# Projections moved behind the mixers, with the head norms inside them; first queries inside the output norms; the recurrence's vector work in halves

## The reference

```python
def _merge_ab(m, o, a, norm_w, w_out):                # end of layer 0's mixer
    hm = _head_norm(m, norm_w).astype(o.dtype) * jax.nn.sigmoid(o)
    cat = jnp.concatenate([hm, a.reshape(a.shape[0], a.shape[1], A_Q)], -1)
    return cat @ w_out
def _merge_c(h, g, norm_w, w_out):                    # end of layer 1's mixer
    return (_head_norm(h, norm_w).astype(g.dtype) * jax.nn.silu(g)) @ w_out
...
x = _layernorm(DEEPNORM_ALPHA * x + g1 * y_lat, ln_w[layer, 0], ln_b[layer, 0])
f_lat = _peer(x * (1.0 + sc2) + sh2, ...)             # its queries: q = hb @ wq
...
def rg_lru_mixer(zb, conv_w, conv_b, w_r, b_r, w_i, b_i, lam):
    ...
    log_a = -LRU_C * r.astype(jnp.float32) * jax.nn.softplus(-lam.astype(jnp.float32))
    a = jnp.exp(log_a)
    inp = jnp.sqrt(-jnp.expm1(2.0 * log_a)) * (i * xb).astype(jnp.float32)
    ...                                                # h = a * h_before + inp, along the tokens
    return jax.nn.gelu(gate) * h.astype(gate.dtype)
def ssd_mixer(...):
    xbc = jax.nn.silu(causal_dwconv(xbc, conv_w, conv_b))
```

## Time and profile before

| | value |
|---|---|
| median of 3 runs | 3676.08 us (3673.44 to 3679.04) |
| profiled execution / its span | 3676.99 / 3675.2 us |
| mean granted clock of TensorE | 0.938 |
| PE busy | 3006.5 us, 82% |
| DVE busy | 1954.0 us, 53% |
| ACT busy | 830.8 us, 23% |
| POOL busy | 880.6 us, 24% |
| DMA | 1024.09 MB, mean 279 GB/s; 403 to 427 GB/s in the bulk of the PEER layers |

### The profile page before, as it was taken

How to read it: one execution, slowest core, us unless ns; L and a number is a source line. 1 busy time by engine, 2 the same in 40 slices (tenths; PEclk the granted TensorE clock), 3 DMA queues, 4 the chain that set the end, 5 groups by cost and what they waited for, 6 DMA issues and landing times. The chain is left out here.

```text
span 3675.2 us, 28126 instructions
## 1 busy us (share of the span) xinstructions
PE 3006.5 (82%) x8564; PEld 1485.9 (40%) x8564; DVE 1954.0 (53%) x5001; ACT 830.8 (23%) x2149; POOL 880.6 (24%) x773
## 2 busy tenths in 40 slices
PE   6997788888888888777888777888877779898898
PEld 3443443333333333333343543333332536453663
DVE  1136657777777777677710756777776331222101
ACT  0112412222222222222312512222222130121100
POOL 0000004444444444444400004444444000000000
PEclk8997799999999999999999889999999899898999
DMA  5143129999999999999922439999999333333343
GB/s 200 58 147 129 63 92 427 427 427 426 427 427 423 423 423 420 424 421 417 403 97 92 156 135 427 427 427 426 427 427 411 133 126 119 106 115 115 115 148 115
DMA packets 242859, 1024.09 MB, mean 279 GB/s; under 512 B 46582, under 2 KB 51190, under 8 KB 142342
## 3 DMA queue, kind: packets, MB, share of 16 engines
q0 software_dynamic: 110592, 805.36, 52.2%
q1 hardware_dynamic: 131688, 215.68, 16.7%
q10 hardware_dynamic: 432, 1.31, 0.1%
HBM read 1021.15 MB, written 1.13 MB: 278 GB/s over the span
## 5 line engine op out<-in xcount | busy, mean ns | idle before, releaser
L1526 PE MATMUL l_peer_experts_acc<-l_peer_experts_ring,l_peer_experts_diag 128*128 128x512 f32 x1840 | 866.9, 614 | 208.3 <-ACT l_peer_experts_diag L1584 207.6
L1526 PE MATMUL l_peer_experts_acc<-weight_slots,l_peer_experts_diag 128*128 128x512 f32 x1232 | 588.9, 621 | 152.4 <-ACT l_peer_experts_diag L1584 151.9
L1745 DVE SCALAR_TENSOR_TENSOR l_peer_experts_ring<-l_peer_experts_ring,h_tiles 128x1024 f32<-128x1024 f32 x460 | 563.3, 1225 | 277.5 <-DMA l_peer_experts_ring<-in_expert_rows,l_peer_experts_picks 273.9
L1453 POOL DMA_INDIRECT l_peer_experts_ring<-in_expert_rows,l_peer_experts_picks x460 | 528.7, 1149 | 616.7 <-PE l_peer_experts_acc L1526 540.9
L1453 POOL DMA_INDIRECT weight_slots<-in_expert_rows,l_peer_experts_picks x308 | 350.7, 1139 | 1303.3 <-DVE l_peer_experts_picks L1674 875.0
L1526 PEld LDWEIGHTS l_peer_experts_acc<-l_peer_experts_ring,l_peer_experts_diag 128*128 128x128 f32 x1840 | 340.3, 193 | 703.9 <-issue 406.7
L1745 DVE SCALAR_TENSOR_TENSOR weight_slots<-weight_slots,h_tiles 128x1024 f32<-128x1024 f32 x308 | 377.1, 1224 | 184.0 <-DMA weight_slots<-in_expert_rows,l_peer_experts_picks 180.5
L1526 PEld LDWEIGHTS l_peer_experts_acc<-weight_slots,l_peer_experts_diag 128*128 128x128 f32 x1232 | 230.9, 196 | 487.0 <-issue 282.1
L1577 ACT ACTIVATE l_peer_experts_gel<-l_peer_experts_dots 128x2 f32<-128x2 f32 x384 | 78.2, 204 | 1183.9 <-DVE l_peer_experts_ring L1745 712.0
L1584 ACT ACTIVATE l_peer_experts_diag<-const_ident,l_peer_experts_wgt 128x128 f32<-128x128 f32 x768 | 266.3, 394 | 238.5 <-DVE l_peer_experts_wgt L1691 223.9
L1478 PE MATMUL l_peer_experts_queries<-h_t,l_query_weights 128*128 128x512 f32 (+3 forms) x576 | 182.3, 462 | 4.2 <-PEq L61 4.2
(11 more groups left out here) (459 smaller groups left out, 3336.8 us busy)
## 6 DMA issues: line engine op xcount, KB each, us to landing
weight_slots<-in_w_mod SPq DMA_DIRECT2D x24, 2048.0 KB, 7.6
weight_slots<-in_w_in SPq DMA_DIRECT2D x20, 2048.0 KB, 7.6
l_query_weights<-query_weights SPq DMA_DIRECT2D x16, 1024.0 KB
weight_slots<-in_w_mlp_up SPq DMA_DIRECT2D x8, 2048.0 KB, 7.7
weight_slots<-in_w_mlp_down SPq DMA_DIRECT2D x8, 2048.0 KB, 7.6
weight_slots<-in_gla_w_in SPq DMA_DIRECT2D x6, 2048.0 KB, 7.7
weight_slots<-in_ab_w_in SPq DMA_DIRECT2D x5, 2048.0 KB, 8.8
l_peer_experts_ring<-in_expert_rows,l_peer_experts_picks POOLq DMA_INDIRECT x460
```

Of the source, the lines that this page charges most:

```text
L1453: pool.indirect_dma_start(rows(b, k, None), None, uv, bass.IndirectOffsetOnAxis(ap=picks[:, b % 4, k:k + 1], axis=0)).then_inc(landing(b, ...
L1526: ins = nc.tensor.matmul(acc[:, b % 2, c * BANK:(c + 1) * BANK], diag[:, k % DIAGS, :], row[:, c * BANK:(c + 1) * BANK], start=(k == 0), s ...
L1745: nc.vector.scalar_tensor_tensor(row, row, 1.0, h[:, tile_of(b), :], ALU.mult, ALU.mult, accum_out=dots[:, b % 2, k:k + 1]).then_inc(dotte ...
```

## The change

It does five things.

1. ab_qkv (and its weight tiles) comes behind the mLSTM rather than ahead of it, and carries the mLSTM's head norm as a side (`head_norm_parts`, new, the same operations as `stage_head_norm`). The stage ab_norm is gone. ab_qkv's evictions are now ACT's alone.
2. c_g comes behind the GLA, takes silu in its evictions, and carries the GLA's head norm. Behind its last matmul it multiplies by the gate (four pieces of 512 columns on DVE) and does the 16 transposes and their 4 copies itself. The stages c_norm and c_turn are gone.
3. `stage_out_norm` computes head 0's query for the first token tile (16 matmuls of 128x128 and two copies into a new buffer) ahead of the transposes of the tile before the last but one (layer 0: tile 2 of 4) or of the last (layer 1). `stage_peer` begins with `score(0)`, and `project` at unit 2.
4. The SSD convolution's taps and bias are loaded in b_xbc rather than b_z; SP waits there until they have landed.
5. `lru_parts` takes 1 - a*a = -(a*a + 1) tanh(log_a), so it has no reciprocal, and does all of it in two halves of 4 of the 8 groups. Both roots come ahead of b_za's last eviction; tanh and exp of the first half come one part earlier.

TensorE's list around the end of layer 1's mixer, first before the change, then after. `gla_` is the GLA, `c_g_acc` the gate's projection, `c_turn_` and `c_g_turned` the transposes, `c_out_` the output projection with its norm; a branch ends a stage or opens one.

```diff
-    both = func is None and len(groups(BANK)) > 1 and side is None
+    both = func is None and len(groups(BANK)) > 1 and side is None and turned_out is None
...
+                if turned_out:
+                    for i, (t, m) in enumerate(quads):
+                        pe.wait_ge(made, i + 1)
+                        if i >= 4:
+                            pe.wait_ge(emptied, i - 3)
+                        for k in range(4):
+                            at = t * BANK + k * P
+                            last = nc.tensor.transpose(turn_ps[:, i % 4, k, :], turn_src[:, m, at:at + P], ident)
+                        last.then_inc(turned, 1)
...
+                        act.wait_ge(turned, i + 1)
+                        nc.scalar.activation(turn_dst[:, 4 * t:4 * t + 4, m * P:(m + 1) * P], turn_ps[:, i % 4, :, :], ACT.Copy).then_inc(emptied, 1)
...
+                    make_link = Link(dve, make_chain)
+                    for i, (t, m) in enumerate(quads):
+                        if m == 0:
+                            dve.wait_ge(act_out, t + 3)
+                        make(make_link, m, slice(t * BANK, (t + 1) * BANK)).then_inc(made, 1)
...
+                def query():
+                    wq, wq_loaded, count, _ = queries
+                    pe.wait_ge(wq_loaded, count)
+                    pe.wait_ge(emptied, quads_of(0)[-1] + 1)
+                    pe.wait_ge(gated, n - 1)
+                    for half in range(2):
+                        for k in range(KC):
+                            last = nc.tensor.matmul(acc[:, 0, half, 0:P], wq[:, 0, k, half * P:(half + 1) * P], h_t[:, k, 0:P], start=(k == 0), stop=(k == KC - 1))
+                        last.then_inc(queried, 1)
                 for i in range(max(n - 2, 0), n):
+                    if i == max(n - 2, 1):
+                        query()
                     turn(i)
             @block.scalar
@@ -754,6 +802,11 @@
                     root(i)
                     copy(i - 2)
                 for i in range(max(n - 2, 0), n):
+                    if i == max(n - 2, 1):
+                        for half in range(2):
+                            act.wait_ge(queried, half + 1)
+                            nc.scalar.activation(queries[3][:, 0, half, 0:P], acc[:, 0, half, 0:P], ACT.Copy)
                     copy(i)
...
+    def scalar(act):
+        if gate is not None:
+            for m in tiles:
+                nc.scalar.activation(gate[:, m, :], gate[:, m, :], gate_func).then_inc(gated, 1)
+        for i in range(len(tiles)):
+            act.wait_ge(ss_ready, i + 1)
+            nc.scalar.activation(rs[:, i, :], ss[:, i, :], ACT.Sqrt).then_inc(rs_ready, 1)
...
+    return {"sync": sync, "scalar": scalar, "vector": vector}, normed
...
-                first_head = project(0, before, 1)
-                for _ in range(2):
-                    next(first_head)
+                pe.sem_inc(q_done, 2)
+                first_head = project(2, before, 1)
                 score(0)
...
-                take(0, 4)
+                act.sem_inc(q_taken, 2)
+                take(2, 4)
...
+def early_conv_parts(nc, st, w, b, wc, bc):
+    loaded = st.sem("conv_loaded")
+    def sync(sp):
+        load_conv(sp, w, b, wc, bc, loaded)
+        sp.wait_ge(loaded, 80)
+    return [{"sync": sync}]
...
-        dve.wait_ge(tanh_ready, 1)
-        link(nc.vector.tensor_scalar(den[:, :, :], th[:, :, :], -1.0, 1.0, ALU.mult, ALU.add))
-        link(nc.vector.reciprocal(den[:, :, :], den[:, :, :]))
-        nc.vector.scalar_tensor_tensor(th[:, :, :], th[:, :, :], -2.0, den[:, :, :], ALU.mult, ALU.mult).then_inc(root_in, 1)
-        dve.wait_ge(root_out, 1)
-        link(nc.vector.tensor_tensor(i_t[:, :, :], i_t[:, :, :], th[:, :, :], ALU.mult))
...
+        def logs(g):
+            dve.wait_ge(emptied, HALF * (g + 1))
+            for h in range(HALF * g, HALF * g + HALF):
+                last = nc.vector.tensor_scalar(r[:, h, :], r[:, h, :], cols[:, 4, h:h + 1], None, ALU.mult)
+            last.then_inc(loga_ready, 1)
+            link(nc.vector.tensor_tensor(some(i_t, g), some(i_t, g), some(x, g), ALU.mult))
+        def squares(g):
+            dve.wait_ge(a_ready, g + 1)
+            link(nc.vector.tensor_tensor(some(den, g), some(r, g), some(r, g), ALU.mult))
+            dve.wait_ge(tanh_ready, g + 1)
+            nc.vector.scalar_tensor_tensor(some(th, g), some(den, g), 1.0, some(th, g), ALU.add, ALU.mult).then_inc(root_in, 1)
+        def scans(g):
+            dve.wait_ge(root_out, g + 1)
+            link(nc.vector.tensor_tensor(some(i_t, g), some(i_t, g), some(th, g), ALU.mult))
+            for h in range(HALF * g, HALF * g + HALF):
+                last = nc.vector.tensor_tensor_scan(den[:, h, :], r[:, h, :], i_t[:, h, :], 0.0, ALU.mult, ALU.add)
+            link(last)
+            link(nc.vector.tensor_tensor(some(gate, g), some(gate, g), some(den, g), ALU.mult))
+        logs(0)
+        squares(0)
+        logs(1)
+        squares(1)
+        scans(0)
+        scans(1)
+    g0, g2, g4, g6 = (gates(h) for h in range(0, GROUPS, 2))
+    return [{"sync": sync, "scalar": decay}, g0, g2, g4, {"tensor": g6["tensor"], "scalar": lambda act: (g6["scalar"](act), powers(0)(act))},
+            {"scalar": powers(1), "vector": vector}, {"scalar": root(0)}, {"scalar": root(1)}]
...
-    some(a["ab_w_in"][0], ("ab_v", 2 * M_W, M_W), ("ab_qk", 0, 2 * M_W), ("ab_o", 3 * M_W, M_W), ("ab_qkv", qkv, A_Q + 2 * A_KV))
+    some(a["ab_w_in"][0], ("ab_v", 2 * M_W, M_W), ("ab_qk", 0, 2 * M_W), ("ab_o", 3 * M_W, M_W))
     some(a["w_mod"][0], ("mod0_rest", 2 * D, 4 * D))
+    some(a["ab_w_in"][0], ("ab_qkv", qkv, A_Q + 2 * A_KV))
...
-            stage_linear(nc, "ab_qkv", weights, h_t, tiles, qkv)
             stage_mlstm(nc, qk_t, v_aug, g_cols, m_rows, consts["sel"], consts["far"], hm, weights, (*mod0, mod_out))
+            stage_linear(nc, "ab_qkv", weights, h_t, tiles, qkv,
+                         side=lambda st: [head_norm_parts(st, hm, range(TT), H_M, P, a["ab_norm_w"][0], cat, LN_EPS, o, ACT.Sigmoid)[0]])
             stage_attention(nc, qkv, consts["cos"], consts["sin"], consts["bars"], a["ab_sink"][0], consts["ident"][:, :], cat, weights, (*mod1, mod_out))
-        stage_head_norm(nc, "ab_norm", hm, range(TT), H_M, P, a["ab_norm_w"][0], o, ACT.Sigmoid, cat, LN_EPS, weights)
-        stage_transpose(nc, "ab_turn", consts["ident"][:, :], cat, h_t, range(TT), KC)
+        stage_transpose(nc, "ab_turn", consts["ident"][:, :], cat, h_t, range(TT), KC, weights=weights)
...
-            stage_linear(nc, "c_g", weights, lat_t, token_tiles(LT), g)
             stage_gla(nc, wl, up, bias, h_t, q_t, k_t, v, consts["sees"], consts["ident"][:, :], *scratch, hc, weights, (*mod1, mod_out))
-        stage_head_norm(nc, "c_norm", hc, range(LT), H_C, DV_C, a["gla_norm_w"][0], g, ACT.Silu, hc, LN_EPS, weights)
-        stage_transpose(nc, "c_turn", consts["ident"][:, :], hc, h_t, range(LT), KC)
+        def gated(link, m, cols):
+            return nc.vector.tensor_tensor(hc[:, m, cols], hc[:, m, cols], g[:, m, cols], ALU.mult)
+        stage_linear(nc, "c_g", weights, lat_t, token_tiles(LT), g, func=ACT.Silu,
+                     side=lambda st: [head_norm_parts(st, hc, range(LT), H_C, DV_C, a["gla_norm_w"][0], hc, LN_EPS, weights=weights)[0]],
+                     turned_out=(gated, hc, h_t, consts["ident"][:, :]))
...
+                                     + early_conv_parts(nc, st, a["ssd_conv_w_2"][0], a["ssd_conv_b_2"][0], *conv))
```

133 lines of the change are left out of this document (91 added, 42 removed).

## The result

The changed kernel's four runs took 3620.86, 3623.09, 3632.12 and 3632.14 us, median 3627.61, against 3676.31 for four runs of the kernel before: a ratio of 0.9866 (95% interval 0.9845 to 0.9887). Four more runs of it in a later series gave 3618.09 to 3629.40 (ratio 0.9853, 0.9836 to 0.9869). Forecast were 3616.4 us and a range of 3605 to 3629. So it is faster, as said, and the size is 49 us where 60 were forecast. The profiled execution, 3620.86 us with a span of 3619.1, is the second shortest of the eight, so all_again's profile further down is the fairer picture of the usual execution.

The account below looks back on a forecast made before the run. PE is 82% busy, but its idle gaps at stage starts and ends were taken as the cost. Gains sum to 59.7 us, from 3677.0 to 3617.3 profiled, 3616.4 for the median; range 3605 to 3629.

Parts of the forecast that it names:

- ab_qkv behind the mLSTM, 13.3: Attention's end to ab_turn: removing ab_norm, its head norm hidden under ab_qkv's matmuls, gains 13.3 us, bounds 11 to 15.
- 0.4 of half clock: Cost of 0.4 us counted against the moved ab_qkv for running at half clock.
- c_g behind the GLA, 11.0: GLA's end to c_out: norm, gate and transposes inside the moved c_g, gaining 11.0 us, bounds 9 to 14.
- c_out's own start then falls 0.7 short in clock: Start of c_out after the moved c_g: 0.7 us lost to a lower clock.
- First queries, 4.6 and 4.6: Starts of both PEER layers: head 0's query computed inside the output norms gains 4.6 us in each layer.
- Taps a stage earlier, 7.9 and 1.0: Convolution beside b_z: earlier start gains 7.9 us, and b_g's start after a shorter idle 1.0 more.
- Recurrence, 17.3: Tail ahead of b_wb: no reciprocal, work in halves; gains 17.3 us, bounds 15 to 18.5.
- DVE then ends at about 3014: Recurrence's tail: DVE's last work ends at about 3014, with the last eviction ending at 3013.0.
- (a): Rival, PEER layers: gathers set the ends, so the earlier first score gives nothing; 3625.6 us, chance 0.08.
- (b): Rival, recurrence: ACT's single queue makes PE or DVE wait, so the tail remains; 3631 us, chance 0.05.
- (c): Rival, b_xbc: the taps' element loads delay SP's weight loads or the gated MLP's; 3620 to 3625 us, chance 0.06.
- (d): Rival, moved ab_qkv and c_g: PE stays at clock 0.50, matmuls take twice as long; 3681 us, slower, chance 0.03.

Follow-up runs that it names:

- all_again: The changed kernel run once more with nothing edited: median 3627.34 us, profiled execution 3629.40 us.
- undo_ab: The changed kernel with ab_qkv ahead of the mLSTM and ab_norm a stage of its own, as before: 3636.82 us.
- late_only: The changed kernel with ab_qkv, c_g and first queries all undone, keeping only the recurrence and the earlier taps: 3655.54 us, ratio 0.9937 to the kernel before.
- undo_gate: The changed kernel with c_g ahead of the GLA and c_norm and c_turn as stages of their own, as before: 3634.06 us.
- undo_queries: The changed kernel with head 0's first queries computed in both PEER layers again, as before: 3635.08 us.
- best: logs_first plus, in layer 0, a second early query for token tile 1 in ab_out and the first exp ahead of the copies: 3618.76 us, ratio 0.9833.
- undo_taps: The changed kernel with the convolution's taps and bias loaded in b_z, as before: 3630.98 us.
- logs_first: The changed kernel with both halves' logarithms on DVE ahead of the first half's squares: 3621.29 us, ratio 0.9853 to the kernel before.
- before_again: The kernel before, unchanged, run and profiled a second time: 3677.17 us over ten runs, ratio 1.000.

## Why the prediction was right, and where a term was mis-sized

The mechanism of each of the five edits was right and four of their own gains came close. Most of the shortfall of 11 us is in the clock of stages that the change doesn't touch, which the prediction allowed for in its range (5 us either way) but had at nothing in its sum; 1.9 are the recurrence's. That the total still lies in the range is owed to that allowance, not to having sized it.

1. *ab_qkv behind the mLSTM, 13.3.* The 14.7 of ab_norm went, as the 2.05 us show. The term itself was sized well: 12.5 to 14.2, in the mean 13.0, once the stages that the edit leaves alone are taken out (undo_ab). All but ab_qkv gives 13.8, less than 1 us off the 14.7; ab_qkv itself is at 44.2 to 44.6 us in eight of ten profiles where it was 43.2, and at 42.9 in two, so the "0.4 of half clock" was 1.0 to 1.3 in most and nothing in some. What was missing stands beside the term: the stretch as a whole gains 14.5 and 7.5 in the two profiles of the changed kernel, since in all ten the mLSTM is 1.7 to 5.0 longer. late_only and undo_ab, with the longest one (89.6) in the old order, show that this doesn't come from the order.
2. *c_g behind the GLA, 11.0.* 38.7 against 38.8 worked out, 12.1 of gain up to c_out (10.5 against undo_gate, the GLA left out). The step "c_out's own start then falls 0.7 short in clock" was too small: c_out without the query (undo_queries) takes 42.0 rather than 40.3, 1.7. That makes 10.4. Since this cost and the query's don't add (undo_gate), the split between this term and the next is one choice of two; together c_out is 3.4 longer, where 2.1 to 2.7 were forecast. The windows of its start, before and changed:

```profile
2137.00:2141.00 4.00, 3.24 (x8) 1.59 (x9) 0.00 (x0) 1.28 (x1) 0.00 (x0) 1.00 0.51 182
```

```profile
2110.00:2114.00 4.00, 3.25 (x4) 1.36 (x5) 0.00 (x0) 1.28 (x1) 0.00 (x0) 0.61 1.05 385
```

It begins at 1.00 behind a long idle and 16 transposes that ran at 0.50 (2132.6 to 2136.4), and at 0.61 behind c_g's matmuls and 16 transposes, which ran at 1.00 (2104 to 2109). In these two, how busy PE was and at what clock does not tell how the next stage starts.
3. *First queries, 4.6 and 4.6.* Measured 4.7 and 4.2. That the 4.6 and 4.7 of layer 0 agree so well is luck in part: single profiles with the early query run from 1331.4 to 1337.4, and the changed kernel's own gained 2.0. The longer wait (5.62 us) was foreseen, and so was its cause, half clock at the 384-column query's start (0.51 from 512.5 to 517.0): it took 12.7 us rather than 10.5. best computes the second tile's query early too and puts exp ahead of the copies. On transposes and the clock the windows of c_out say this, ahead of the query and in it:

```profile
2145.00:2148.00 3.00, 1.97 (x9) 1.63 (x9) 2.93 (x3) 2.70 (x6) 0.00 (x0) 0.51 0.00 0
...
2148.00:2153.00 5.00, 5.00 (x28) 5.00 (x29) 2.68 (x3) 0.28 (x1) 0.00 (x0) 0.61 0.01 3
```

The clock is 0.51 behind an idle of 3.40 us and with eight transposes in the window, and 0.61 through the query. So the query did cost 5.67 us and not 5.1, as by the rule of the Trainium skill (TensorE: Matmul & The Clock Gate, Part 4: PE-mode transpose); but with the idle time ahead of it this doesn't show that transposes don't count, and ab_turn's climb from 0.50 to 1.00 still stands against the rule. The same holds for c_out in the kernel before, at 1.00 though the 16 transposes 1.46 us ahead of it ran at 0.50.
4. *Taps a stage earlier, 7.9 and 1.0.* 9.2 in the stage, of which 1.6 are b_z's own matmuls (29.1 rather than 30.7 us, at the better clock); seven variants that keep the edit have b_z at 30.5 to 30.8 and gain 7.4 to 8.1 there. 0 to 2.5 come behind it, and 0.4 go back in b_xbc against undo_taps. The prediction misread one row on the way: 18.45 is how long ACT had been idle at 3087.19, not how far into the stage that is; b_xbc's matmuls began at 3065.09, 22.1 us earlier by the trace. The slack was larger than it said, so nothing hung on it.
5. *Recurrence, 17.3.* 15.4. The step that failed is "DVE then ends at about 3014", that is, 1 us past the eviction; it ended 3.05 past it. The estimate shortened each pass and left out the order: DVE's first squares stand ahead of the second half's logarithms, for which ACT's tanh waits. logs_first removes that and gets 3.2 more, 18.7 in all, just past the forecast's upper bound.

Where the rest went is plainest in all_again, 12 us short of the forecast by its profile. The mLSTM has 5.0 of them, c_q to c_v 2.3, the recurrence 1.9, b_wb to b_z 1.8, ab_qkv's term 0.6, c_out 1.0 and the time ahead of ab_v 0.9; b_z to b_wa gave 2.5 more than forecast, and the other stretches make up the rest. In the changed kernel's own profile, 3.6 short, the mLSTM has only 1.7, ab_o is 1.4 shorter than before, and the last stretch gives 1.5.

Most of these are a start that loses or keeps about 1.7 us. In b_wa and b_wc the sum stays near 60.3 whichever of them has it (31.0 + 29.4 in the changed kernel, 32.5 + 27.7 in undo_ab), and so in c_k and c_v (29.4 + 55.2, 27.7 + 56.9), where the kernel before has it in neither. What decides it stays open.

Undone one at a time, the edits cost 3.6 to 9.7 us in the runs' medians, 37 in all, against 49 for the whole; by their own stretches they come to more than 50. The medians hold the other stages' changes of clock too, so the sizes above rest on the profiles.

Of the rivals, (a) falls by undo_queries, (b) by the eviction being on time, (c) by SP's rows in b_xbc:

```profile
3035.27 1.36 SPq L2209 DMA_DIRECT2D b_sconv_b<-in_ssd_conv_b  x1
3044.52 0.37 SPq L115 DMA_DIRECT2D weight_slots<-in_w_in  x1
```

The bias, last of the five loads, has landed at 3036.6, 7.9 us before the first weight load is due. b_xbc grew 0.8, of which undo_taps gives back 0.4. (d) falls: c_g with all that is in it took 33.2 us, ab_qkv 42.9 to 44.6, and twice 27.5 and 41.2 would have been 55 and 82.

## What to carry to other kernels

A stage that leaves the matrix engine idle can be given to a projection that has free vector time; here the gain could be read off ahead from the idle rows to within 1 or 2 us. When a chain over two engines is cut in halves, write down the order on each engine and follow which half each waits for: the passes' lengths alone missed 3 us here. And ask of every stage behind a change, touched or not, at what clock it starts: a start lost or kept was worth about 1.7 us for most stages here, up to 5 for the mLSTM, so let the range lean to that side where the kernel before starts them well.

## What the runs showed of the hardware

The kernel before is steady: two profiles agree within 0.3 us in all but two of the fourteen stretches (2.8 and 0.5), and the ten runs of before_again lie within 8.5 us. All twelve profiles of the changed kernel and its variants, one of which has the order of before through the first two layers, have the mLSTM's first 16 us at a clock of 0.79 to 0.89 rather than 1.00. Seven of them start c_k at 0.57 to 0.61, where the kernel before starts it at 1.00; in the other five c_v is the one that takes 1.7 us more. Some stages start better instead: ab_o at 1.00 in the changed kernel and 0.74 before, b_g at 1.00 and 0.50. Two executions of one and the same kernel can differ by 7 us in stages whose instructions are the same (386.1 and 393.2 from ab_v to ab_turn). And b_wb, behind the same idle time (2.99 and 2.96 us), started at 0.50 in one variant and at 1.00 in another. Which way a start falls wasn't found.
